# Latents' attention on one core: maxima over thirds of the keys, value products regrouped, scores moved out in four pieces

## The reference, cut to what matters

```python
def attend(q, k, v):
    ...
    scale = hd ** -0.5

    def one_block(qblk):
        s = jnp.einsum('bqkgd,blkd->bkgql', qblk, k).astype(jnp.float32) * scale
        p = jax.nn.softmax(s, axis=-1).astype(v.dtype)
        return jnp.einsum('bkgql,blkd->bqkgd', p, v)
```

## Time and profile before

| | us |
|---|---|
| median of 3 runs | 2715.0 |
| lowest and highest | 2713.01, 2715.04 |
| the profiled execution, its own time | 2714.14 |
| its span in the trace | 2712.3 |
| TensorE busy in the span | 2565.8 (95%) |
| VectorE busy in the span | 1645.7 (61%) |
| ScalarE busy in the span | 1193.8 (44%) |

### The profile page before, as it was taken

One profiled execution on the slowest core, in us unless ns is written; L12 is line 12 of the kernel. 1 busy time (PEld: TensorE's weight loads), 2 busy tenths in 40 slices (PEclk: granted clock), 3 DMA queues, 4 the chain that ended last, 5 costly groups with the idle time before them and its releaser, 6 DMA issues.

```text
span 2712.3 us, 37077 instructions
## 1 busy us (share of the span) xinstructions
PE 2565.8 (95%) x15039; PEld 1926.0 (71%) x15039; DVE 1645.7 (61%) x2459; ACT 1193.8 (44%) x1950; POOL 235.9 (9%) x259
## 2 busy tenths in 40 slices
PE   7999799999899999999999999997799999999994
PEld 3444499999788677575767888884577777777773
DVE  2555677777333345757566344556676776777774
ACT  3311334444333233434343333342576766666663
POOL 1111100000000000000001000000010110101012
PEclk8999899999899999999999999998899999999997
DMA  9310000000101200101012200525688897988887
GB/s 320 135 66 32 0 1 1 1 1 1 63 32 51 96 16 1 55 1 55 1 39 82 78 32 32 190 98 186 236 289 309 281 329 271 312 305 289 305 274 221
DMA packets 176603, 345.01 MB, mean 127 GB/s; under 512 B 9338, under 2 KB 37580, under 8 KB 176434
## 3 DMA queue, kind: packets, MB, share of 16 engines
q1 hardware_dynamic: 166396, 314.09, 32.6%
q0 software_dynamic: 9472, 28.32, 4.1%
q10 hardware_dynamic: 566, 0.24, 0.0%
HBM read 304.35 MB, written 38.27 MB: 126 GB/s over the span
## 4 chain that ended last, share of the span: by engine, by line
PE 63%; issue 22%; DMA 8%; DVE 5%; ACT 1%; POOL 0%; POOLq 0%; DVEq 0%; SPq 0%; ACTq 0%
PE ps L1004 16%; PE ps L228 8%; DMA ffn_scratch<-WK 6%; PE ps L1358 6%; PE ps L751 5%; PE ps L1310 5%; PE ps L779 4%; PE ps L1905 4%; DVE WK L848 2%; PE ps L1421 2%; PE ps L1404 1%; PE ps L1324 1%; PE ps L2448 1%; PE ps L1381 1%; PE ps L1931 1%
## 5 line engine op out<-in xcount | busy, mean ns | idle before, releaser
L2527 ACT ACTIVATE RWr<-R 128x1024 fp32r<-128x1024 f32 x384 | 377.8, 1055 | 71.9 <-PE ps L2448 69.3
L2622 DVE TENSOR_TENSOR W_low<-R,RWr 128x1024 fp32r<-128x1024 f32 x256 | 301.4, 1219 | 84.5 <-ACT RWr L2527 82.4
L2448 PE MATMUL ps<-RWr,R1r 128*128 128x512 f32 x1024 | 329.6, 396 | 6.0 <-DVE R1r L2610 4.3
L1004 PE MATMUL ps<-W_high,tile_high 128*128 128x512 f32 x640 | 251.2, 392 | 7.7 <-DVE W_low L1082 7.2
L1004 PE MATMUL ps<-W_low,tile_high 128*128 128x512 f32 x640 | 250.6, 392 | 0.0
L1004 PE MATMUL ps<-W_high,tile_low 128*128 128x512 f32 x640 | 250.5, 391 | 0.0
L228 PE MATMUL ps<-RW,R 128*128 128x512 f32 (+1 forms) x640 | 248.9, 542 | 0.0
L2448 PEld LDWEIGHTS ps<-RWr,R1r 128*128 128x128 f32 x1024 | 192.9, 188 | 58.2 <-issue 14.2
L228 PEld LDWEIGHTS ps<-RW,R 128*128 128x128 f32 x640 | 119.2, 191 | 105.4 <-issue 101.5
L1074 DVE TENSOR_TENSOR tile_low<-R,tile_high 128x1024 fp32r<-128x1024 f32 x80 | 97.9, 1223 | 156.9 <-ACT tile_high L1030 156.7
L2622 DVE TENSOR_TENSOR tile_high<-R,RWr 128x1024 fp32r<-128x1024 f32 x128 | 150.8, 1219 | 29.8 <-ACT RWr L2527 29.5
(11 more groups left out here) (346 smaller groups left out, 4638.1 us busy)
## 6 DMA issues: line engine op xcount, KB each, us to landing
R<-in_w_dram SPq DMA_DIRECT2D x96, 2048.0 KB, 13.3
RW<-in_w_in_dram SPq DMA_DIRECT2D x11, 1024.0 KB, 5.4
R<-in_w_mod_dram SPq DMA_DIRECT2D x5, 2048.0 KB, 12.8
RW<-in_w_in_dram SPq DMA_DIRECT2D x5, 2048.0 KB, 8.4
RW<-in_w_mod_dram SPq DMA_DIRECT2D x4, 2048.0 KB, 11.3
WK<-in_w_mod_dram SPq DMA_DIRECT2D x3, 2048.0 KB, 7.8
mix_scratch<-R SPq DMA_DIRECT2D x10, 512.0 KB, 2.6
R<-mix_scratch SPq DMA_DIRECT2D x10, 512.0 KB, 7.0
```

What stands on the lines that cost most here:

```text
L1004: i = pe.matmul(bank(m % 4), Tsplit[a][:, m % 2, k, :], Wsplit[b][:, k, :], start=(k == 0 and n == 0), stop=(k == KD - 1 and n == 2))
L2448: m = pe.matmul(bank(bank_of(e, i, j)), stat[a][:, k, :], w[b][:, k % 2, :], start=(k == 0 and z == 0), stop=(k == KD - 1 and z == 2))
L2527: act.activation(ring_high[n % RING], pair_raw[i][j][:, 2 * q:2 * q + 2, :], ACT.Copy).then_inc(S("weights_high"), 1)
L2622: dve.tensor_tensor(ring_low[n % RING], pair_raw[i][j][:, 2 * q:2 * q + 2, :], ring_high[n % RING].bitcast(F32), ALU.subtract).then_inc(S( ...
```

## The change

Three things are changed, all of them in the latents' turns.

- **Maxima over thirds.** `scores` is called three times, for 4 blocks each, and raises `scores_done` three times in a turn. `top_of` takes the maxima of 4 blocks (1024 columns) at a time. After the second third VectorE combines the two results, after the third one it combines again.
- **Value products regrouped.** 7, 5 and 12 value products stand ahead of `turn_max`, between it and `spread_max`, and behind `spread_max`, where 8, 7 and 9 stood.
- **Four pieces.** `shift` moves out 2, 2, 4 and 4 blocks where it moved 4, 4 and 4. The next turn's scores wait at blocks 0, 2, 4 and 8. The exponentials stay in three pieces, and the first of them waits for the first two pieces.

```diff
-        top_halves = [WK[:, 768 + n * 256:1024 + n * 256] for n in range(2)]
+        top_thirds = [WK[:, 768 + n * 256:1024 + n * 256] for n in range(2)]
...
+        PIECES = ((0, 2), (2, 4), (4, 8), (8, 12))
...
-                for b in range(6 * half, 6 * half + 6):
-                    if u and b % 4 == 0:
-                        pe.wait_ge(S("kept_by_dve"), CTX_K + 3 * (u - 1) + b // 4 + 1)
+                for b in range(4 * third, 4 * third + 4):
+                    for p_, (lo, hi) in enumerate(PIECES):
+                        if u and b == lo:
+                            pe.wait_ge(S("kept_by_dve"), CTX_K + 4 * (u - 1) + p_ + 1)
...
                 if 0 <= v < len(turns):
-                    weigh_rows(v, 0, range(0, 8))
+                    weigh_rows(v, 0, range(0, 7))
                 if u < len(turns):
                     turn_max(u)
                 if 0 <= v < len(turns):
-                    weigh_rows(v, 0, range(8, 12))
-                    weigh_rows(v, 1, range(0, 3))
+                    weigh_rows(v, 0, range(7, 12))
                 if u < len(turns):
                     spread_max(u)
                 if 0 <= v < len(turns):
-                    weigh_rows(v, 1, range(3, 12))
+                    weigh_rows(v, 1, range(0, 12))
...
-            def top_of(u, half):
-                dve.wait_ge(S("scores_done"), CTX_K + 2 * u + half + 1)
-                o = half * 3 * BANK
-                ch(dve.tensor_reduce(top_halves[half], ps[:, o:o + 3 * BANK].rearrange("p (b n) -> p n b", n=2 * P), AX, ALU.max))
-                if half:
-                    dve.tensor_tensor(top_halves[1], top_halves[0], top_halves[1], ALU.max).then_inc(S("max_ready"), 1)
+            def top_of(u, third):
+                dve.wait_ge(S("scores_done"), CTX_K + 3 * u + third + 1)
+                o = third * 2 * BANK
+                ch(dve.tensor_reduce(top_thirds[min(third, 1)], ps[:, o:o + 2 * BANK].rearrange("p (b n) -> p n b", n=2 * P), AX, ALU.max))
+                if third == 1:
+                    ch(dve.tensor_tensor(top_thirds[0], top_thirds[0], top_thirds[1], ALU.max))
+                elif third == 2:
+                    dve.tensor_tensor(top_thirds[1], top_thirds[0], top_thirds[1], ALU.max).then_inc(S("max_ready"), 1)
...
-                for p_ in range(3):
-                    dve.tensor_tensor(pT[u % 2][:, 4 * p_:4 * p_ + 4, :], ps[:, p_ * 2 * BANK:(p_ + 1) * 2 * BANK].rearrange("p (b n) -> p b n", b=4),
-                                      shifts.unsqueeze(1).broadcast_to([P, 4, 2 * P]), ALU.add).then_inc(S("kept_by_dve"), 1)
+                for lo, hi in PIECES:
+                    dve.tensor_tensor(pT[u % 2][:, lo:hi, :], ps[:, lo * 2 * P:hi * 2 * P].rearrange("p (b n) -> p b n", b=hi - lo),
+                                      shifts.unsqueeze(1).broadcast_to([P, hi - lo, 2 * P]), ALU.add).then_inc(S("kept_by_dve"), 1)
...
             def exps_of(u, p_):
-                act.wait_ge(S("kept_by_dve"), CTX_K + 3 * u + p_ + 1)
+                act.wait_ge(S("kept_by_dve"), CTX_K + 4 * u + p_ + 2)
```

More of the change, by code:

```diff
@@ L682, in queries_read @@
             else:
-                eng.wait_ge(S("scores_done"), CTX_K + 2 * (turns.index((T, g, 1)) + 1))
+                eng.wait_ge(S("scores_done"), CTX_K + 3 * (turns.index((T, g, 1)) + 1))
         def tile_scores(pe, T, k):
@@ L736, in pe_attn, with scores @@
                 weigh(T_CTX - 1, 3, b)
-            def scores(u, half):
+            def scores(u, third):
                 T, g, hp = turns[u]
-                if half == 0:
+                if third == 0:
                     if hp == 0:
@@ L761, in turn_max @@
                 for a in range(2):
-                    m = pe.transpose(ps[:, 6 * BANK + a * P:6 * BANK + (a + 1) * P], top_halves[1][:, a * P:(a + 1) * P], ident[:, :])
+                    m = pe.transpose(ps[:, 6 * BANK + a * P:6 * BANK + (a + 1) * P], top_thirds[1][:, a * P:(a + 1) * P], ident[:, :])
                 m.then_inc(S("turned_for_dve"), 1)
@@ L785, in turn_rows @@
                 pe.wait_ge(S("kept_by_act"), CTX_K + u + 1)
-                pe.wait_ge(S("kept_by_dve"), CTX_K + 3 * min(u + 2, len(turns)))
+                pe.wait_ge(S("kept_by_dve"), CTX_K + 4 * min(u + 2, len(turns)))
                 for a in range(2):
@@ L793, in pe_attn @@
                 if u < len(turns):
-                    scores(u, 0)
-                    scores(u, 1)
+                    for third in range(3):
+                        scores(u, third)
                 if u >= 2:
@@ L870, in dve_attn @@
                 if u < len(turns):
-                    top_of(u, 0)
-                    top_of(u, 1)
+                    for third in range(3):
+                        top_of(u, third)
                     negate(u)
@@ L945, in act_attn @@
                     if u:
-                        act.wait_ge(S("kept_by_dve"), CTX_K + 3 * u)
+                        act.wait_ge(S("kept_by_dve"), CTX_K + 4 * u)
                     keep_max(u)
```

## The result

| | before | after |
|---|---|---|
| median, us | 2715.0 (5 runs, 2713.01 to 2716.8) | 2727.11 (5 runs, 2723.03 to 2727.33) |
| ratio, 95% interval | | 1.0041 (1.0027 to 1.0056) |
| profiled execution, span | 2712.3 | 2721.2 |

The changed kernel is slower by about 0.4%, 12 us. The forecast was 2714.1, no change, with a range up to 2717.5: it was wrong, outside its range, and on the side that had been given 0.07. The profiled execution of the changed kernel is the fastest of its five (2723.03).

The account below looks back on a forecast made before the run. TensorE was taken as nearly full in the steady turns, with gaps to win. A turn stays 11.23 against 11.227 us; -0.7 at the start, -0.3 at the end and +0.1 over 30 turns give 2714.1 us, range 2709.5 to 2717.5.

Parts of the forecast that it names:

- the side that had been given 0.07: Measured time slower than 2720.4 us: the slow rival and half of "something else", chance 0.07.
- Thirds: From first score to transposes: 6.61 us with maxima over thirds instead of 6.85, a gain of 0.24 a turn.
- The section on bounds: Opening of the prediction: in the steady turns TensorE is nearly full, busy 325.49 of 337.00 us; the change can win its gaps.
- The slow rival: VectorE's loop becomes the bound: pieces lose their overlap, loop 11.46 us, 30 turns lose 7, 2721; chance 0.06.
- the 0.04: Chance given to "something else" than the forecast and the named rivals, half on each side.
- Regrouping: From transposes to next scores: 4.63 us instead of 4.37, costing 0.26 a turn, with a new 0.12 wait at the spreading product.
- the first rival: The spreading product doesn't wait: turn 11.11 us, 30 turns win 3.6, 2710.5; chance 0.13.
- Pieces: Moved scores: first piece ends 1.3 us ahead of the scores, ending their wait; four pieces take 3.47, 0.07 more, hidden.
- A turn: Sum of one steady turn: 6.61 + 4.63 = 11.24 us, 11.23 unrounded, against 11.227 before.
- The start: Between turns 0 and 1: scores start earlier, transposes of turn 1 at 345.86 against 346.59, -0.7 us.
- The end: Behind the last turn: the inversion and L789 come 0.3 us earlier.
- The clock's rival: TensorE's shorter rest behind the last turn, 3.2 us, keeps the clock at 2.4 GHz: 2.3 us more won, 2711.8; chance 0.12.

Follow-up runs that it names:

- e1: The changed kernel with GpSimd's subtraction cut to 2 of 512 columns in the latents' tiles: 2713.87 us.
- e9: The changed kernel with GpSimd's subtraction waiting until VectorE has made the diagonal of the turn in which it ran until then, nothing left out: 2714.53 us.
- e11: The changed kernel (thirds, four pieces) with value products in groups of 10, 6 and 8 and GpSimd's subtraction moved away from the combinations by a wait: 2707.73 us.
- e3: The kernel before with only the value products regrouped to 7, 5 and 12; halves and three pieces stay: 2722.05 us.
- e2: The changed kernel with GpSimd's subtraction behind one more wait, which was already met when GpSimd came to it: 2725.74 us.
- e5: The changed kernel with GpSimd's subtraction behind a wait one count higher than in e2, also already met: 2725.24 us.
- e4: The kernel before with only the maxima over thirds; 8, 7, 9 value products and three pieces stay: 2730.14 us.

## Why the prediction was wrong

**The step that failed** is in "Thirds": "The combination (0.43, with 0.04 between chained instructions...)". It took the price of an operation on two SBUF tensors from one row (L850), where GpSimd was at rest, and put it at an earlier place in the turn without asking who else is at work there. The runs showed 1.11 us in its place in 13 of the 30 turns and 1.38 in one; away from GpSimd it takes 0.42, as forecast (e1, e9). The row that answers it, GpSimd's at 501.29, was in the trace. It stands 5.90 behind the start of the move ahead of it:

```profile
495.39 3.48 DVE L862 TENSOR_TENSOR R<-ps,WK 128x1024 f32<-128x1024 f32 x3 [1.59 <-ACT WK L924]
```

In the prediction's sum the move starts at 2.62 and the first score at 4.63, so the subtraction starts 5.90 - 2.01 = 3.89 behind the first score and lasts 1.27, and the added combination would start at 4.40: they meet. With 14 subtractions this makes 13 x 0.69 + 0.96 = 9.9 us. The section on bounds named TensorE, VectorE, ScalarE and the DMAs and left out GpSimd, whose 17.74 us of work in 337 stand in the row that it quotes. None of the rivals had this mechanism. The slow rival had the right sign and the wrong place: VectorE's pieces kept their overlap (four pieces of 0.69, 0.68, 1.22 and 1.22 in 3.55 together, as forecast), and its loop was shorter than said (by 0.12 in e11, which it bounds), not longer. Its 0.06 and half of the 0.04 make 0.08, not 0.07.

**The rest of the sum held**, and e9, in which nothing but the collision is missing, and e1 measured 2714.53 and 2713.87 against the forecast 2714.1. That they agree to 0.4 is in part luck: the executions of e9 lie between 2711.26 and 2718.95.

- *Thirds*: a maximum of 1024 columns takes 1.22 to 1.23, the last one follows the combination at once (399.56 behind 399.10 + 0.42). The turns of e1 (11.225) are 0.25 shorter than those of e3 (11.478), which has the same groups of products, halves and three pieces; the sum had 0.24 for the thirds and nothing for the pieces there. Right.
- *Regrouping*: 0.26 a turn; e3 alone gives 11.478 - 11.227 = 0.25. The wait at the spreading product was real, though no idle is noted ahead of L771 as the prediction had asked: its weight load starts at 379.57, 1.41 behind the transposes as in the sum, and its two passes last 0.70 where they took 0.60 in the earlier trace rows. The value products behind it start 1.95 behind the transposes and the second score stands at 4.74, as in the sum (1.95, and 4.63 + 0.12). So the first rival is out.

```profile
378.16 0.44 PE L764 MATMUL ps<-ident,WK 128*128 128x128 f32 x2 [0.34 <-DVE WK L853]
378.43 1.28 PE L781 MATMUL ps<-WK,RW 128*128 128x129 f32 x10
379.57 0.70 PE L771 MATMUL ps<-WK 128*128 128x256 f32 x2
380.11 2.84 PE L781 MATMUL ps<-WK,RW 128*128 128x129 f32 x24
...
382.90 0.28 PE L753 MATMUL ps<-W_low,R3r 128*128 128x256 f32 x1
```

```profile
379.57 0.30 PEld L771 LDWEIGHTS ps<-WK 128*128 128x128 f32 x2
```

- *Pieces*: the move starts at 380.78, 2.62 behind the transposes, and is through at 384.25, 6.09 behind (2.62 and 6.09 in the sum). Alone they win 3.3 by the medians, 0.09 a turn. Right.
- *A turn*: 11.23 forecast, 11.225 in e1, 11.233 in e9. Right.
- *The start*: L857 of the first two turns are 12.54 apart, 12.92 before, so 0.38 is won where the sum had 0.49 (346.59 - 345.86 = 0.73, less the 0.24 by which the first transposes come earlier).
- *The end*: TensorE's rest behind the last turn is 3.18 (3.2 forecast). The clock's rival came halfway: the clock still fell to half, but came back sooner (0.51 from 698 to 700 us, 1.00 from 702), and the 48 passes take 6.71 against 7.74 in the earlier trace rows, 1.0 us of the 2.3.

```profile
698.50 0.69 PE L791 MATMUL ps<-ident,WK 128*128 128x128 f32 x2 [3.18 <-ACT WK L939]
698.98 6.71 PE L781 MATMUL ps<-WK,RW 128*128 128x129 f32 x48
```

**What stays open.** The medians of the changed kernel and of e1 are 13.2 us apart, the long turns explain 9.9. Two further kernels with the changed kernel's timing (e2, e5) came out at 2725.7 and 2725.2, 11.6 above e1. In the traces the rest is not in the attention: from L857 of the first turn to the end of ScalarE's last L923 the changed kernel takes 375.9 us and e1 365.9, 10.0 apart. Other stages scatter, though nothing in them was changed. The first L857 (L854 before) starts between 329.8 and 335.7 us in the fourteen traces. From the first product of one later stage (L1358 in the kernel before) to that of another (L1905) six traces show 692.7 to 693.1 us, the kernel before among them (692.9), and eight show 695.5 to 695.8, the changed kernel (695.8) and e1 (695.7) among them. What sets these two times stays open, and whether the collision costs another 1 to 3 us outside the turns was not settled.

## What to carry to other kernels

A price read off a row holds for the place where the row stands. When an operation on two SBUF tensors is added to VectorE or moved there, look for GpSimd's instructions on SBUF in the same stretch, however idle GpSimd is in all; where they meet, give the one with slack a wait that keeps it away. Here that gave back all of the loss (2714.53); a form with one SBUF input is not held either, but took 0.27 longer in every turn (2722.01). And finer steps pay only where the engine that makes them has room. The regrouping lost 0.25 a turn, as could be read from the rows. The thirds gave 0.10 a turn in the short turns of e4 and 0.25 with the change's groups (e1 against e3), and lost 0.25 with the groups of 10, 6 and 8, where VectorE is the bound. More value products ahead of the transposes won.

## What the runs showed of the hardware

- A combination of two SBUF tensors on VectorE that meets GpSimd's 128x512 subtraction on SBUF takes as long as if it did no work until 0.14 us before the end of GpSimd's row and then its usual 0.42: 1.11, 1.14, 1.47 and 1.03 us in four arrangements and 1.38 at the one odd turn. The profile shows it as busy time of VectorE, with no idle and no releaser, so no list of waits names it.
- An overlap of 0.13 us with the end of GpSimd's row cost nothing. A reduction with one SBUF input (0.69) was not held, and neither were operations on a PSUM and an SBUF tensor (L612, 0.35).
- The kernel before has what looks like the other direction, in a later stage. GpSimd's small L1612 takes 0.19 in most of its 40 instructions, and also under a VectorE operation that reads PSUM and SBUF (L1628). Where it starts 0.1 behind the start of one on two SBUF tensors (L1631) it takes 1.11, and ends with it. No run tested this.

```profile
1104.15 1.22 DVE L1631 TENSOR_TENSOR_SCAN WK<-carry,WK 128x512 f32<-128x512 f32 x1
```

```profile
1104.26 1.11 POOL L1612 TENSOR_SCALAR st<-st 128x1 f32<-128x1 f32 x1
```

- VectorE starts an instruction that waits for nothing 0.08 us before the one ahead has ended, across kinds too (a maximum behind a reciprocal). The four moved pieces are together 0.25 us shorter than the sum of their rows. One that waits for the instruction ahead of it starts 0.03 to 0.04 behind its end (387.18 behind 385.92 + 1.23).
